# Encoder layer with grouped experts on one core: the last routed tile's down products, the late loads and the closing layer norm in another order

## The reference

```python
h = silu(x @ w_gate[e]) * (x @ w_up[e])          # 16 experts of 256 hidden values, two of them per token
h = h * gates[..., None]
y = einsum('nef,efd->nd', h, w_down)             # 256 -> 1024
shared = (silu(x @ ws_gate) * (x @ ws_up)) @ ws_down
x = layer_norm(ALPHA * x + y + shared, ln2_g, ln2_b)    # over the 1024 values of a token
```

## Time and profile before

| what | value |
|---|---|
| median of three runs | 1217.03 us |
| the profiled execution: its own time | 1218.3 us |
| the profiled execution: its span | 1216.4 us |
| TensorE busy | 1200.7 us, 99% of the span |
| VectorE, ScalarE, GpSimd busy | 724.8, 591.5, 218.7 us |
| granted TensorE clock, mean | 0.997 of 2.4 GHz |

### The profile page before, as it was taken

The page is one execution under the profiler, slowest core; times in us unless marked ns, Lnnn a source line. Parts: engine busy times, 40 slices in busy tenths (PEclk is TensorE's granted clock), DMA queues, the critical chain, the costliest instruction groups (busy, mean ns, idle before and its releaser), DMA issues.

```text
span 1216.4 us, 22118 instructions
## 1 busy us (share of the span) xinstructions
PE 1200.7 (99%) x8040; PEld 1077.8 (89%) x8040; DVE 724.8 (60%) x1796; ACT 591.5 (49%) x1463; POOL 218.7 (18%) x276
## 2 busy tenths in 40 slices
PE   9999999999999999999899999999999999999998
PEld 9998888888888888888778888899989999999895
DVE  3222455655565556555767878668856556656358
ACT  4332344544454445444552434244556756766556
POOL 1121001200120012001211122000224423432223
PEclk9999999999999999999989999999999999999999
DMA  9787674365436643667745333493899999999994
GB/s 274 225 302 227 155 196 101 79 165 136 101 80 153 149 101 79 156 164 217 259 140 220 124 122 125 162 360 124 265 335 286 286 287 264 282 295 272 350 311 188
DMA packets 164676, 246.93 MB, mean 203 GB/s; under 512 B 41536, under 2 KB 111424, under 8 KB 163776
## 3 DMA queue, kind: packets, MB, share of 16 engines
q1 hardware_dynamic: 149408, 190.72, 51.5%
q0 software_dynamic: 11776, 41.95, 14.0%
q10 hardware_dynamic: 3408, 13.16, 2.7%
HBM read 150.59 MB, written 65.31 MB: 177 GB/s over the span
## 4 chain that ended last, share of the span: by engine, by line
PE 71%; issue 13%; DVE 5%; DMA 5%; POOL 3%; ACT 1%; POOLq 1%; ACTq 0%; SPq 0%; DVEq 0%
PE bank L916 15%; PE bank L918 15%; PE bank L917 15%; PE bank L1049 9%; PE bank L1036 5%; PE bank L1027 4%; PE bank L1028 3%; PE bank L910 3%; DMA raw_gu<-in_w_up 2%; DMA acc_scratch<-slab,dstc 1%; POOL c_work L2527 1%; DVE w_gu_lo L2180 1%; DVE c_work L2073 1%; DVE c_work L2071 1%; POOL Q L2554 1%
## 5 line engine op out<-in xcount | busy, mean ns | idle before, releaser
L1523 ACT ACTIVATE b_work<-b_work 128x256 f32<-128x256 f32 (+3 forms) x288 | 148.1, 514 | 232.6 <-DVE b_work L1976 232.5
L916 PE MATMUL bank<-xgT_hi,w_gu_hi 128*128 128x224 f32 (+1 forms) x704 | 195.8, 278 | 0.9 <-DVE xgT_lo L2031 0.5
L918 PE MATMUL bank<-xgT_hi,w_gu_lo 128*128 128x224 f32 (+1 forms) x704 | 194.8, 277 | 0.0
L917 PE MATMUL bank<-xgT_lo,w_gu_hi 128*128 128x224 f32 (+1 forms) x704 | 194.7, 277 | 0.0
L1985 DVE COPY b_work<-bank 128x256 f32<-128x256 f32 (+2 forms) x256 | 112.7, 440 | 117.3 <-PE bank L1036 116.3
L916 PEld LDWEIGHTS bank<-xgT_hi,w_gu_hi 128*128 128x128 f32 x704 | 135.0, 192 | 3.2 <-DVE xgT_lo L2031 1.4
L917 PEld LDWEIGHTS bank<-xgT_lo,w_gu_hi 128*128 128x128 f32 x704 | 135.0, 192 | 0.7
L918 PEld LDWEIGHTS bank<-xgT_hi,w_gu_lo 128*128 128x128 f32 x704 | 135.0, 192 | 0.0
L2554 POOL CAST Q<-Q 128x512 fp32r<-128x512 f32 x48 | 53.4, 1143 | 431.5 <-DVE w_k_lo L1915 225.8
L1036 PE MATMUL bank<-keep,b_work 128*128 128x128 f32 x608 | 114.7, 274 | 3.1 <-ACT b_work L1523 3.1
L1036 PEld LDWEIGHTS bank<-keep,b_work 128*128 128x128 f32 x608 | 79.4, 139 | 36.4 <-ACT b_work L1523 7.8
(11 more groups left out here) (247 smaller groups left out, 2831.6 us busy)
## 6 DMA issues: line engine op xcount, KB each, us to landing
raw_gu<-in_w_gate SPq DMA_DIRECT2D x32, 512.0 KB, 8.8
raw_gu<-in_w_up SPq DMA_DIRECT2D x32, 512.0 KB, 9.6
raw_d<-in_w_down SPq DMA_DIRECT2D x16, 1024.0 KB, 9.7
Q<-stage_hi SPq DMA_DIRECT2D x96, 128.0 KB, 2.4
Q<-stage_lo SPq DMA_DIRECT2D x96, 128.0 KB, 2.4
o_scratch<-b_work SPq DMA_DIRECT2D x36, 264.0 KB, 3.3
wo_scratch<-a_work POOLq DMA_DIRECT2D x16, 512.0 KB, 4.6
w_o<-wo_scratch SPq DMA_DIRECT2D x16, 512.0 KB, 5.8
```

Source lines behind the costliest of these rows:

```text
L916: nc.tensor.matmul(o, w_hi, x_hi, start=first, stop=False)
L917: nc.tensor.matmul(o, w_hi, x_lo, start=False, stop=False)
L918: return nc.tensor.matmul(o, w_lo, x_hi, start=False, stop=last)
L1523: nc.scalar.activation(prob[:, u % 2, 0:n], prob[:, u % 2, 0:n], ACT.Exp, scale=-1.0, bias=o[:, HD:HD + 1], accum_out=o[:, HD + 1:HD + 2])\
```

## The change

- SyncE: the loop over routed tiles ends one round sooner, and the round is written out behind it with `load_late(0)` ahead of it. The two vectors of the last layer norm are loaded behind the last routed tile's down weights, once the shared gate and up weights are split. The wait for the first late step's products stands only before the sums of tile 8.
- TensorE: the down products of R are made after quarter 0 of the first late step, where it was quarter 1; their first half waits for the down weights' low part by fourths (`by_parts`).
- `Z_ORDER` is 0 to 11, where 5 stood after 7.
- ScalarE: `z_stats(2)` goes ahead of the second late step's silu, `z_stats(3)` behind it; the third late step has 4, 5, 6, 7; only 8 and later stay behind the steps.
- VectorE: `z_out(1)` and `z_out(2)` go ahead of `gated` of the second late step, `z_out(3)` behind it; the third late step has `z_out(4)` and `z_out(5)` ahead of `gated`. The first centring half of tile 6 goes behind the third late step, and there `add_shared` stands first. `z_out(5)` is gone from the end.

```diff
-        Z_ORDER = (0, 1, 2, 3, 4, 6, 7, 5, 8, 9, 10, 11)
+        Z_ORDER = tuple(range(TILES))
...
-            with sp.Fori(0, more * 2 + 3) as j:
+            with sp.Fori(0, more * 2 + 2) as j:
                 load_gu(j + 1)
                 load_d(j)
+            sp.wait_ge(S["gx_made"], EARLY + 2)
+            load_late(0)
+            load_gu(more * 2 + 3)
+            load_d(more * 2 + 2)
             for half in range(2):
                 wait("wg_lo", (more * 2 + 4) * KD + (KD // 2 + KD // 2 * half))
                 load_raw_gu(ws_gate, ws_up, half)
-            sp.wait_ge(S["gx_made"], EARLY + 2)
-            load_late(0)
             load_d(more * 2 + 3)
+            wait("wg_lo", (more * 2 + 6) * KD)
+            sp.dma_start(ln2g, ln2_g.partition_broadcast(P)).then_inc(S["ln2_loaded"], 16)
+            sp.dma_start(ln2b, ln2_b.partition_broadcast(P)).then_inc(S["ln2_loaded"], 16)
             wait("gx_made", more * 2 + (EARLY + 4))
             load_late(1)
             load_late(2)
             wait("wd_lo", more * 8 + 20)
             load_raw_d(ws_down)
-            wait("wg_lo", (more * 2 + 6) * KD)
-            sp.dma_start(ln2g, ...)
-            sp.dma_start(ln2b, ...)
...
-            wait("gx_made", more * 2 + (EARLY + 5))
             for t in Z_ORDER:
+                if t == 2 * EARLY + 2:
+                    wait("gx_made", more * 2 + (EARLY + 5))
                 sp.dma_start(base[:, t, :], acc_t[t]).then_inc(S[f"rows_ld{t}"], 16)
...
+                        if by_parts:
+                            pe.wait_ge(S["wd_lo"], (q - (EARLY - 1)) * 4 + (2 * k + c + 1))
...
                 def first_late(f):
-                    if f == 1:
+                    if f == 0:
                         for half in range(2):
-                            ddn(q - 1, 1 - s, half, n - 1)
+                            ddn(q - 1, 1 - s, half, n - 1, half == 0)
...
                     z_stats(1)
+                    z_stats(2)
                 if last:
-                    for t in (3, 4, 6, 7):
+                    for t in (4, 5, 6, 7):
                         z_stats(t)
...
                 if n == LATE0 + 1:
-                    z_stats(2)
+                    z_stats(3)
...
-            for t in (5, 8):
-                z_stats(t)
+            z_stats(8)
...
                 if last:
-                    for t in (2, 3, 4):
-                        z_out(t)
+                    z_out(4)
+                    z_out(5)
...
                     z_out(0)
+                    z_out(1)
+                    z_out(2)
                 gated(q, s, n)
-                if last:
-                    z_centre_half(6, 0)
                 if n == LATE0 + 1:
-                    z_out(1)
+                    z_out(3)
...
+            add_shared(end - 1, EARLY + LATE - 2, 1)
+            z_centre_half(6, 0)
             z_centre_half(6, 1)
             z_scale_half(6, 0)
-            add_shared(end - 1, EARLY + LATE - 2, 1)
...
             add_shared(end, EARLY + LATE - 1, 1)
-            z_out(5)
```

More of the change, by code:

```diff
@@ L860, in load_gu, with load_late @@
                     load_raw_gu(w_gate[e], w_up[e], half)
-            with sp.Fori(0, more * 2 + 3) as j:
+            def load_late(n):
+                for part in range(2):
+                    sp.dma_start(plain(xg_of(LATE0 + n)[part][:]), t_d[n, part]).then_inc(S[f"late_ld{n}"], 16)
+            with sp.Fori(0, more * 2 + 2) as j:
                 load_gu(j + 1)
                 load_d(j)
+            sp.wait_ge(S["gx_made"], EARLY + 2)
+            load_late(0)
+            load_gu(more * 2 + 3)
+            load_d(more * 2 + 2)
             for half in range(2):
@@ L869, in _ @@
                 load_raw_gu(ws_gate, ws_up, half)
-            def load_late(n):
-                for part in range(2):
-                    sp.dma_start(plain(xg_of(LATE0 + n)[part][:]), t_d[n, part]).then_inc(S[f"late_ld{n}"], 16)
-            sp.wait_ge(S["gx_made"], EARLY + 2)
-            load_late(0)
             load_d(more * 2 + 3)
+            wait("wg_lo", (more * 2 + 6) * KD)
+            sp.dma_start(ln2g, ln2_g.partition_broadcast(P)).then_inc(S["ln2_loaded"], 16)
+            sp.dma_start(ln2b, ln2_b.partition_broadcast(P)).then_inc(S["ln2_loaded"], 16)
             wait("gx_made", more * 2 + (EARLY + 4))
@@ L882, in _ @@
             load_raw_d(ws_down)
-            wait("wg_lo", (more * 2 + 6) * KD)
-            sp.dma_start(ln2g, ln2_g.partition_broadcast(P)).then_inc(S["ln2_loaded"], 16)
-            sp.dma_start(ln2b, ln2_b.partition_broadcast(P)).then_inc(S["ln2_loaded"], 16)
             for half in range(2):
@@ L1254, in dgu, with ddn @@
                         after(f)
-            def ddn(q, s, half, n):
+            def ddn(q, s, half, n, by_parts=False):
                 if half == 0:
                     pe.wait_ge(S["h_lo"], q + 1)
-                    if n == 0 or EARLY <= n <= LATE0:
+                    if (n == 0 or EARLY <= n <= LATE0) and not by_parts:
                         pe.wait_ge(S["wd_lo"], 4 if n == 0 else (q - (EARLY - 2)) * 4)
```

## The result

| | before | after |
|---|---|---|
| median | 1217.03 us | 1229.99 us |
| times | 1216.11 to 1219.99 (5) | 1226.79, 1227.44, 1229.99, 1230.13, 1230.27 |
| ratio, 95% interval | | 1.0094 [1.0081, 1.0107] |
| profiled execution: time, span | 1218.3, 1216.4 | 1226.79, 1224.9 |

The two medians lie 13.0 us apart; by the ratios the changed kernel is 11.4 and 11.8 us slower, and the text goes by the ratios. 6.7 was forecast, and the range (to 1225.5) does not hold the result. The sign and both places were as forecast. The stall was longer than forecast, and a cost of TensorE's clock was missing.

What follows compares the result with a forecast made beforehand. TensorE, busy for 99% of the span, was taken as the bound. A 3.0 us stall before R plus 3.7 us for the order gave 6.7 us on the median 1217.03: 1223.7 us, range 1217.5 to 1225.5.

Steps and rivals of the forecast that it cites:

- They push the last weights out of a quiet stretch: Late rows move R's last weights into 1110 to 1116, where GpSimd's gather and scatter fill 94.4% of the engines.
- a stall of 3.0 us: TensorE waits before R's products for weights 10.3 us later; bounds 0 and 5.4 us.
- some gaps they will fill: R's weights use gaps in GpSimd's traffic, so 10.3 us later was taken, not the upper 12.7.
- Rival (c): R's weights come last of all on the DMA engines: stall 5.4 us, time 1226.1; chance 0.08.
- All later TensorE work shifts by it: Everything TensorE does behind the stall before R, scatters included, moves later by the stall's 3.0 us.
- The order of moments and outputs: Before the last down products, VectorE's added work starts them 3.7 us later; bounds 3.1 and 4.3.
- The vectors sooner: Vectors ahead of the other late rows leave R-1's scatter at 11.55 us; bounds 0.5 worse, 5.3 better.
- The quarter sooner: R's down products move 2.85 us sooner without gain, as their reader waits for R-1's scatter; bounds 0 and 1.6.
- the sums' rows without a wait: SyncE's removed wait before the sums was hidden behind the scatter's landing: 0, at most 0.1 us.
- rival (b): Not slower: R-1's scatter lands up to 5.3 us sooner in an emptier queue; 1219.1 or 1216.1; chance 0.20.
- the floor: TensorE's one wait before the last down products, 0.95 us, is all a perfect order of the tail could give back.
- The turns of the packets: DMA engines serve queues packet by packet, so R's 1 KB weight packets get little time beside 4 KB scatter packets.

Runs made afterwards that it cites:

- e9: The changed kernel run again unaltered, against the kernel before: 1227.11 to 1230.49 us, ratio 1.0097.
- e2: The kernel before with only the first late rows (2 MB) put ahead of R's last weights: 1224.1 us, ratio 1.0055.
- e10: e2 with twenty unused products put into TensorE's wait before R's transposes: 1222.88 us, ratio 1.0043 against the kernel before.
- e1: The kernel before with only the new order of tiles, moments and outputs: 1220.1 us, ratio 1.0023.
- e6: The changed kernel with the first late rows back in their old place, against the kernel before: 1221.73 us, ratio 1.0038.
- e8: e7 with the new order of tiles, moments and outputs added, against the kernel before: 1222.35 us, ratio 1.0034.
- e11: The kernel before with the offset products of banks 2 and 3 moved ahead of the last down products: 1217.98 us, ratio 1.0003.
- e4: The kernel before with only the high part (1 MB) of the first late rows ahead of R's weights: 1218.12 us, ratio 1.0009.
- e3: The kernel before with only the sooner quarter, the sooner vectors and the moved sums' wait: 1217.05 us, ratio 1.0002.
- e7: The kernel before with the sooner quarter, the moved sums' wait and the last late rows issued behind the vectors: 1217.3 us, ratio 1.0002.
- e14: The kernel before with the sooner quarter, moved sums' wait and last late rows behind the sums' first two rows, old orders: 1217.04 us, ratio 0.9991.
- e5: The changed kernel with the first late rows right behind R's weights, against the kernel before: 1221.26 us, ratio 1.0035.

## Why the prediction was wrong

**The place of the stall, right; its size, the step that failed first.** "They push the last weights out of a quiet stretch" is what happened: the weights' packets met gather and scatter, and ScalarE's split waited 5.03 us for them. The term was "a stall of 3.0 us". I had reckoned the last weights 10.3 us later; against a trace that runs 1.8 ahead, 1121.97 is 12.7 later than 1111.1, which is the upper bound, where all of GpSimd's packets go ahead. The stall measured 5.24 in after, 4.9 in e9 and 5.4 in e2: 2.2 us of the miss. I had taken a value below the bound because "some gaps they will fill". SyncE's issue of R's third weight load took 5.72 us, and the fourth could be issued only at 1104.84; that this cost anything is not shown, since SyncE's queue alone took 102.0% of the engines in 1104 to 1110. Rival (c) had this stall, and I gave it 0.08.

**A term that the sum lacks: TensorE's clock.** "All later TensorE work shifts by it" takes the stall's length for its cost. Behind the stall the clock was granted at 1.2 GHz, and the transposes for R and down products of R-2 were made at half the rate: 2.3 to 2.4 us more in the traces of after and, by e10's filling, of e2. The trace of before has no fall of the clock in the expert stage, where TensorE never waits over 0.95 us, but it has one elsewhere, behind a stretch in which TensorE was not full, which the forecast did not use (windows of before):

```profile
608.00:614.00 6.00, 4.80 (x34) 4.06 (x34) 4.81 (x19) 3.50 (x10) 2.89 (x3) 1.00 0.38 127
614.00:620.00 6.00, 5.02 (x18) 4.23 (x18) 2.12 (x7) 3.47 (x13) 0.89 (x2) 0.55 0.92 267
620.00:626.00 6.00, 6.00 (x39) 5.48 (x38) 4.89 (x19) 2.74 (x9) 0.00 (x0) 0.88 0.09 31
```

From it the term could have been bounded before the run: 0.45 and 0.12 of full speed missing in two windows of 6 us, 3.4 us of full-speed work. It is a bound and not the cost, since part of the low stretch falls into the stall itself: in after the same windows lack 0.42 and 0.14, 3.4 us too, and 2.3 were paid.

**The order of moments and outputs: 3.7 forecast.** From the landing of tile 1's sums it is 4.4 in after, just over the upper bound of 4.3. From `z_out(1)` to the last down products VectorE waits for the reciprocal roots three times, 1.5 us in all, where I had put one wait of 0.6 (VectorE's timeline of after):

```profile
1183.24 1.28 DVE L2446 SCALAR_TENSOR_TENSOR raw_gu<-d_work,keep,raw_gu 128x1024 f32<-128x1024 f32 x1 [0.78 <-POOL keep L2679]
...
1186.40 1.29 DVE L2446 SCALAR_TENSOR_TENSOR raw_gu<-d_work,keep,raw_gu 128x1024 f32<-128x1024 f32 x1 [0.51 <-POOL keep L2679]
...
1189.82 1.28 DVE L2446 SCALAR_TENSOR_TENSOR raw_gu<-d_work,keep,raw_gu 128x1024 f32<-128x1024 f32 x1 [0.18 <-POOL keep L2679]
```

But the starting point was off the other way. The 6.75 us of tile 1's load in the earlier trace rows are 4.6 in after, as in e1, e6 and e8, and I had kept them. They are not one execution's chance: e11 has 6.7 and e4 6.3. But e2, e3, e7 and e10, with the old order too, have 4.5 to 4.9; what makes this load longer in three kernels stays open. Counted from the issue of that load, the last down products start 28.4 us behind it in before and 30.7 in e1 and in after: 2.3, and with the clock's fall (1.6) and the shorter tail (0.7), 3.2 in e1's trace; 2.8 timed. So alone the order costs less than forecast. Together with e3's edits it costs 4.6 (e6).

**The vectors sooner: 0, with 0.5 worse as a bound.** The scatter of R-1 took 12.65 to 12.91 us instead of 11.55, 1.1 to 1.4 longer, over the bound. Alone nothing is lost by it (e3), where tile 1's load took 2.2 less and TensorE's last wait is only 0.2; with the orders in, it is on the path, and e6 is 1.8 us above e1 by ratio, 1.1 in the traces.

**Right.** The quarter sooner and the sums' rows without a wait changed nothing (e3). The scatter of R-1 was issued into the same late rows and did not land sooner in after. Of rival (b), e7 and e14 show why it could give next to nothing even with an emptier queue: e14 takes away TensorE's last waits, and the gain of 1.1 by ratio is about the 0.95 us that I had set as the floor. The turns of the packets held: 155 to 157 and 145 to 145 in after, and with GpSimd's four times as large the weights were late by the upper bound. The Trainium skill has these turns as a rule ("DMA: Bandwidth & Descriptors", section "Queues, rings and completion order"), and the trace agrees with it.

**The sum with what was measured.** In the profiled executions it is 10.3, against 6.7 forecast: the stall 2.2 more, the clock 2.4, the scatter of R-1 1.1, the order 0.7, the load of tile 1 2.1 less, the tail 0.7 less; 3.6 in all. In times: late rows 6.7 (e2), orders with e3's edits 4.6 (e6): 11.3, against 11.4 timed.

## What to carry to other kernels

When an edit puts bytes ahead of weights on a queue that shares the DMA engines with gathers and scatters, reckon the lateness at its upper bound, subtract the slack once, and expect nothing while it stays inside it: here 1 MB ahead cost nothing that could be told, 2 MB cost 6.7 us. In every trace with the stall it cost more than its length, unless TensorE was kept at work (e10), and the spacing of the products behind it says how much. And an order of small pieces that is laid against the landing of a load must be judged together with that landing: the same orders cost 2.8 to 4.6 us or nothing that could be told, by when the sums land and what is issued ahead of them.

## Not expected of the hardware

- The granted clock fell to 1.2 GHz in e2, e9 and after around a wait of 4.9 to 5.4 us of an otherwise full TensorE, and in e1, e5, e6 and e8 behind one of 2.38 to 2.44 us; in the profiled executions of after and e9 waits of 2.42 and 2.38 us at the same place were followed by a clock of 1.00. The length of the wait alone does not say whether it falls.
- Twenty products that nobody reads kept the clock at 1.00 through the same wait (e10).
- One DMA issue held SyncE for 5.72 us (after, 1099.02), while the neighbours took 0.4 to 2.2 us. The same issue took 5.47 in e2 and 5.41 in e10, and 0.98 in before.
- Packets of two queues went one for one, 1 KB beside 4 KB (145 and 145 in 1116 to 1119 of after, 144 and 146 in e9, 145 and 147 in 1119 to 1122 of e2).
